# Two kinds of small copies in the ConvGLU stage move from ScalarE to VectorE

## The reference: what is computed

```
def conv_glu(h, prev, p):
    u = h @ p['w_up']                       # (rows, 2 * 2816)
    L = u.shape[1]
    pad = jnp.concatenate([prev, u], axis=1)
    c = p['conv_b'] + p['conv_w'][0] * pad[:, 0:L]
    for j in range(1, CONV_W):              # CONV_W = 3
        c = c + p['conv_w'][j] * pad[:, j:j + L]
    a, g = jnp.split(c, 2, axis=-1)
    return (jax.nn.silu(g) * a) @ p['w_down'], pad[:, -(CONV_W - 1):]
```

## Time and profile before

| what | value |
|---|---|
| median of 3 runs | 2471.32 us (2468.33 to 2472.02) |
| the profiled execution: its time | 2468.33 us |
| its span, first to last instruction | 2466.5 us |
| mean granted clock of TensorE | 0.981 |
| TensorE busy | 2352.0 us, 95% |
| VectorE busy | 1094.4 us, 44% |
| ScalarE busy | 990.8 us, 40% |
| POOL busy | 864.8 us, 35% |

### The profile page before, as it was taken

One profiled execution on the slowest core, in us unless ns is written; L12 is line 12 of the kernel. 1 busy time (PEld: TensorE's weight loads), 2 busy tenths in 40 slices (PEclk: granted clock), 3 DMA queues, 4 the chain that ended last, 5 costly groups with the idle time before them and its releaser, 6 DMA issues.

```text
span 2466.5 us, 48737 instructions
## 1 busy us (share of the span) xinstructions
PE 2352.0 (95%) x16832; PEld 2163.7 (88%) x16832; DVE 1094.4 (44%) x1676; ACT 990.8 (40%) x2052; POOL 864.8 (35%) x365
## 2 busy tenths in 40 slices
PE   5999999999999999999989999999999999999998
PEld 4888889999999997898778888899999989978986
DVE  3644463244452564266144544533353525633651
ACT  4544553234223553355244444532342234533542
POOL 3243132235333343344342342232353324434433
PEclk9999999999999899999989999999999999999999
DMA  4132212322222221322212122222122223213322
GB/s 133 62 99 81 69 61 72 97 67 67 84 72 86 70 82 65 94 80 82 82 62 87 61 81 82 72 76 85 60 71 75 81 70 86 76 63 97 86 78 89
DMA packets 239156, 193.52 MB, mean 78 GB/s; under 512 B 7088, under 2 KB 225296, under 8 KB 238960
## 3 DMA queue, kind: packets, MB, share of 16 engines
q1 hardware_dynamic: 217552, 172.38, 22.7%
q10 hardware_dynamic: 21408, 18.55, 2.3%
HBM read 177.49 MB, written 13.42 MB: 77 GB/s over the span
## 4 chain that ended last, share of the span: by engine, by line
issue 65%; POOL 17%; PE 12%; DVE 4%; ACT 2%; POOLq 1%; DVEq 0%; ACTq 0%
POOL wlo L509 13%; POOL rstd L515 3%; PE ps L968 2%; PE ps L614 2%; PE ps L969 2%; PE ps L616 2%; PE ps L970 2%; PE ps L615 2%; DVE ca L1926 2%; PE ps L659 1%; DVE ca L1931 1%; ACT ca L1373 1%; PE ps L960 0%; PE ps L959 0%; DVE ca L1936 0%
## 5 line engine op out<-in xcount | busy, mean ns | idle before, releaser
L509 POOL TENSOR_TENSOR wlo<-raw,whi 128x1024 fp32r<-128x1024 f32 (+2 forms) x322 | 773.4, 2424 | 1518.4 <-ACT whi L1002 1518.4
L614 PE MATMUL ps<-hl,whi 128*128 128x272 f32 x2240 | 650.8, 291 | 8.2 <-DVE mer L1861 4.8
L616 PE MATMUL ps<-hl,wlo 128*128 128x272 f32 x2240 | 646.7, 289 | 0.0
L615 PE MATMUL ps<-hl,whi 128*128 128x272 f32 x2240 | 644.8, 288 | 0.0
L631 PE MATMUL ps<-whi,hl 128*128 128x256 f32 x1792 | 516.5, 288 | 1.7 <-issue 1.0
L632 PE MATMUL ps<-wlo,hl 128*128 128x256 f32 x1792 | 509.0, 284 | 0.0
L633 PE MATMUL ps<-whi,hl 128*128 128x256 f32 x1792 | 508.0, 284 | 0.0
L614 PEld LDWEIGHTS ps<-hl,whi 128*128 128x128 f32 x2240 | 423.9, 189 | 11.8 <-DVE mer L1861 5.0
L616 PEld LDWEIGHTS ps<-hl,wlo 128*128 128x128 f32 x2240 | 422.9, 189 | 0.0
L615 PEld LDWEIGHTS ps<-hl,whi 128*128 128x128 f32 x2240 | 422.5, 189 | 0.0
L1002 ACT ACTIVATE whi<-raw 128x1024 fp32r<-128x1024 f32 (+2 forms) x322 | 311.8, 1016 | 237.2 <-PE ps L970 137.0
(11 more groups left out here) (215 smaller groups left out, 3024.1 us busy)
## 6 DMA issues: line engine op xcount, KB each, us to landing
raw<-in_w_in_dram SPq DMA_DIRECT2D x130, 512.0 KB, 4.6
raw<-in_w_up_dram SPq DMA_DIRECT2D x88, 512.0 KB, 4.8
raw<-in_w_branch_a_dram SPq DMA_DIRECT2D x16, 512.0 KB, 3.9
raw<-in_w_branch_b_dram SPq DMA_DIRECT2D x16, 512.0 KB, 4.4
raw<-in_w_out_dram SPq DMA_DIRECT2D x16, 512.0 KB, 3.9
raw<-in_w_down_dram SPq DMA_DIRECT2D x32, 256.0 KB, 3.8
raw<-in_w_down_dram SPq DMA_DIRECT2D x16, 512.0 KB, 3.7
raw<-in_w_down_dram SPq DMA_DIRECT2D x8, 768.0 KB, 4.5
```

The lines of the kernel that those rows point to most:

```text
L509: ins = e.tensor_tensor(wlo[:, s, a:b], raw[:, s, a:b], whi[:, s, a:b].bitcast(F32), ALU.subtract)
L614: e.matmul(out, wh, hi, start=(c == 0), stop=False)
L615: e.matmul(out, wh, lo, start=False, stop=False)
L616: ins = e.matmul(out, wl, hi, start=False, stop=(c == KC - 1))
```

## The change

`last_rows` and `state_rows` go from ScalarE's program. VectorE makes the same copies with `tensor_copy`: the state columns of unit 0 at the head of the pass, and in every unit, after L1931 and before the wait for tanh, the two last-row copies of unit j and the two state copies of unit j + 1. The waits follow: TensorE's transposes wait for VectorE, ScalarE's first tap waits for VectorE's state copies, and ScalarE's L1432 waits for VectorE's last-row copies of unit j - 2 and no longer for its own instruction before; VectorE's L1915 no longer waits for ScalarE's last-row copies.

```
 def conv_rows():
     acquire("t", dve=1)
-    e.wait_ge(*S.at("act_step", ("cs", FB - 1)))
+    e.wait_ge(*S.at("dve_step", ("cs", FB - 1)))
...
 # ScalarE
         if s == 0:
-            e.wait_ge(*S.at("dve_step", "edges"))
+            e.wait_ge(*S.at("dve_step", ("pads", j)))
...
-    def last_rows(j):
-        e.wait_ge(*S.at("dve_free_" + UP_BANKS[j % 2][3], ("ug", j, 1)))
-        for q in range(2):
-            c0 = SEQ if q == 0 else TOK + 2
-            e.wait_ge(*S.own())
-            e.activation(cs[:, 2 * q:2 * q + 2, :]..., up[:, j % 2, :, c0:c0 + 2], ACT.Copy)
-    def state_rows(j):
-        if j >= 2:
-            e.wait_ge(*S.at("dve_step", ("conv2", j - 2, 1)))
-        for s in range(2):
-            e.wait_ge(*S.own())
-            e.activation(up[:, j % 2, s, SEQ + 2:SEQ + 4], conv[...], ACT.Copy)
...
-    state_rows(0)
-    state_rows(1)
     for j in range(FB):
         ...
             first_tap(j - 1, 1)
-            last_rows(j - 1)
             half_tanh(j - 1)
-            if j + 1 < FB:
-                state_rows(j + 1)
         e.wait_ge(*S.at("mm_ready", ("T", j, 0, 0)))
         if j >= 2:
+            e.wait_ge(*S.at("dve_step", ("cs", j - 2)))
             e.wait_ge(*S.at("dve_step", ("conv2", j - 2, 1)))
-            e.wait_ge(*S.own())
...
     first_tap(FB - 1, 1)
-    last_rows(FB - 1)
     half_tanh(FB - 1)
 # VectorE
+    def pads(j):
+        for s in range(2):
+            e.wait_ge(*S.own())
+            e.tensor_copy(up[:, j % 2, s, SEQ + 2:SEQ + 4],
+                          conv[:, ds(l, 1), 0:2, ds(f * FB + (j + s * FT), 1)].rearrange("p a v c -> p (a v c)"))
+    pads(0)
     for j in range(FB):
         for t in range(2):
             e.wait_ge(*S.at("mm_ready", ("T", j, 1, t)))
-            if t == 0 and j >= 2:
-                e.wait_ge(*S.at("act_step", ("cs", j - 2)))
...
         # after the two L1931
+        for q in range(2):
+            c0 = SEQ if q == 0 else TOK + 2
+            e.wait_ge(*S.own())
+            e.tensor_copy(cs[:, 2 * q:2 * q + 2, :].rearrange("p t (s c) -> p s t c", s=2)[:, :, :, j],
+                          up[:, b, :, c0:c0 + 2])
+        if j + 1 < FB:
+            pads(j + 1)
         e.wait_ge(*S.at("act_step", ("th", j)))
```

More of the change, by code:

```diff
@@ L1374, in first_tap @@
                             *S.up("act_step", key=("tap0", j, s)))
-                    def last_rows(j):
-                        e.wait_ge(*S.at("dve_free_" + UP_BANKS[j % 2][3], ("ug", j, 1)))
-                        for q in range(2):
-                            c0 = SEQ if q == 0 else TOK + 2
-                            e.wait_ge(*S.own())
-                            e.activation(cs[:, 2 * q:2 * q + 2, :].rearrange("p t (s c) -> p s t c", s=2)[:, :, :, j],
-                                         up[:, j % 2, :, c0:c0 + 2], ACT.Copy).then_inc(*S.up("act_step", key=("cs", j) if q else None))
-                    def state_rows(j):
-                        if j >= 2:
-                            e.wait_ge(*S.at("dve_step", ("conv2", j - 2, 1)))
-                        for s in range(2):
-                            e.wait_ge(*S.own())
-                            e.activation(up[:, j % 2, s, SEQ + 2:SEQ + 4],
-                                         conv[:, ds(l, 1), 0:2, ds(f * FB + (j + s * FT), 1)].rearrange("p a v c -> p (a v c)"),
-                                         ACT.Copy).then_inc(*S.up("act_step", key=("pads", j) if s else None))
                     def half_tanh(j):
@@ L1903, in dve_program @@
                     e.wait_ge(*S.own())
-                    e.memset(up[:, :, :, 0:2], 0.0).then_inc(*S.up("dve_step", key="edges"))
+                    e.memset(up[:, :, :, 0:2], 0.0).then_inc(*S.up("dve_step"))
+                    def pads(j):
+                        for s in range(2):
+                            e.wait_ge(*S.own())
+                            e.tensor_copy(up[:, j % 2, s, SEQ + 2:SEQ + 4],
+                                          conv[:, ds(l, 1), 0:2, ds(f * FB + (j + s * FT), 1)].rearrange("p a v c -> p (a v c)")).then_inc(
+                                *S.up("dve_step", key=("pads", j) if s else None))
+                    pads(0)
                     for j in range(FB):
@@ L1933, in dve_program @@
                                 *S.up("dve_step", key=("conv2", j, 1) if v == 2 else None))
+                        for q in range(2):
+                            c0 = SEQ if q == 0 else TOK + 2
+                            e.wait_ge(*S.own())
+                            e.tensor_copy(cs[:, 2 * q:2 * q + 2, :].rearrange("p t (s c) -> p s t c", s=2)[:, :, :, j],
+                                             up[:, b, :, c0:c0 + 2]).then_inc(*S.up("dve_step", key=("cs", j) if q else None))
+                        if j + 1 < FB:
+                            pads(j + 1)
                         e.wait_ge(*S.at("act_step", ("th", j)))
```

## The result

The changed kernel takes 2485.27 us (median of 5 runs, 2481.79 to 2486.53) and the kernel before 2471.32 (5 runs). The ratio is 1.0056, with a 95% interval from 1.0045 to 1.0067: slower by 14 us. The profiled execution has a span of 2482.8 us, 16.3 more than before.

What follows compares the result with a forecast made beforehand. Stage F's ScalarE-VectorE round, longer than TensorE's 12.0 us a unit, bounds the pass. Copies needing 1.06 us in a 0.98 us hole cost 40 x 0.08 = +3.2 us on 2471.3, forecasting 2474.5 us; range 2466 to 2485.

Steps and rivals of the forecast that it cites:

- the sum for the four copies on VectorE: Between L1931 and L1936: copies and gaps need 1.06 us in a hole of 0.98, late by 0.08 a round, +3.2 us.
- Gain 0: ScalarE's removed state copies L1391, 0.76 us per j, lie beside VectorE's L1936 and L1942, so removing them changes nothing.
- What bounds the kernel: Stage F: the ScalarE-VectorE round, averaging 12.75 us, exceeds TensorE's 12.0 a unit, so TensorE waits before the down projection.
- The gains of nothing: On ScalarE: removing copies L1382 (0.45 us per j) and L1391 (0.76 us per j) gains 0 each.
- the reading that L1931 was not waiting for it: VectorE's L1931 starts 0.37 us after the first tap, before the second copy L1382 is over; the profile's naming is attribution.
- My upper bound: VectorE's four copies cost what they cost on ScalarE: 1.29 us, late by 0.31 a round, +12.4 us, 2484.
- such hiccups: Delays of 0.3 to 0.4 us in a few rounds may move when code is added, 2 to 3 us either way.
- The second one, clearly slower: VectorE copies cost as on ScalarE, or wait registers cannot load meanwhile: late 0.12 us or more a round, 2481 to 2484; 28%.
- The clock: Before the down projection: longer waits shift TensorE's slow-clock stretch by a few matmuls, under 2 us over all passes, no term.

Runs made afterwards that it cites:

- e6: Kernel before, with POOL's subtraction of stage F cut in four instructions a unit and not two: 2436.58 us, ratio 0.9867.
- e1: Changed kernel with only the last-row copies moved to VectorE, the state copies staying on ScalarE: 2471.18 us, ratio 0.9999 to before.
- e3: Changed kernel with neither engine making the last-row or state copies: 2476.54 us, ratio 1.0027 to before.
- e2: Changed kernel with only the state copies moved to VectorE, the last-row copies staying on ScalarE: 2475.89 us, ratio 1.0019 to before.
- e5: Kernel before, ScalarE untouched, with four more copies on VectorE at the change's place, into unused buffers: 2478.13 us, ratio 1.0035.
- e8: Changed kernel with the two state copies moved to VectorE's next wait, for ScalarE's copy L1403: 2473.96 us, ratio 1.0008 to before.
- e4: Changed kernel with all four VectorE copies put earlier, into its wait for the first tap of half 1: 2521.31 us, ratio 1.0199 to before.
- e11: Changed kernel with state copies moved to VectorE's wait for L1403, and POOL's stage F subtraction cut in four: 2443.28 us, ratio 0.9889 to before.
- e7: Changed kernel with POOL's subtraction of stage F cut in four instructions a unit: 2468.75 us, ratio 0.9999 to before.

## Why the prediction was wrong

Two steps failed: the sum for the four copies on VectorE, late by 0.08 us a round in the prediction and by 0.32 when measured, and the "Gain 0" for taking L1391 from ScalarE, which was a loss of 0.26 us a round.

**What bounds the kernel: right.** Stage F's round against TensorE's 12.0 us, the lag caught up with at unit 10, 40 rounds that count. Time and mean round go together in nine kernels, and once the round is down to TensorE's 12.0 us the waits vanish (e6).

**The gains of nothing: right for L1382** (e1), and the reading that L1931 was not waiting for it. **Wrong for L1391.** The prediction says "Gain 0" of taking them away, and counts ScalarE's copies by their time alone. They also worked out the address that the first taps use. Without them each first tap is 0.13 us later, +0.26 us a round (e3), less the 0.08 us that VectorE is quicker before L1931 (plain round +0.17 in e2, 7 us). VectorE is 0.09 us quicker before the other half too, but there the next instruction waits for POOL's and gives it back: 2.78 us for 2.68. This term was missing from the sum.

**The sum on VectorE: mis-sized.** I had "2 x (0.035 + 0.147) + 2 x (0.17 + 0.147) + 0.05", 1.05 to 1.06. Measured: the pair of last-row copies 0.03 + 0.38, then 2 x (0.21 + 0.17), then 0.12 to L1925: 1.30. Three parts are larger than I took them: the copies are 0.17 us and not 0.147 (worked out from a copy of one element, 144 ns, and one of 32 in a row, 180, which reads PSUM and not SBUF); the gap before the state copies is 0.21, where the register instruction lasts 129 ns; and behind the last short copy 0.12 us pass, not 0.05. So the hole was overfilled by 0.32 us and not 0.08. My upper bound, ScalarE's own cost, gave 0.31, and this is what VectorE cost. The term alone is 12.8 us; e5 has it by itself (plain round 0.32 - 0.08 = 0.24 expected, 0.26 measured), and e8 shows the same copies free where they fit. The table that the Trainium skill has for VectorE ("VectorE: DVE Perf Modes", on the TRN2 errata) was further off: by an estimate from its 58 cycles 64 ns, against 170. By the same estimate its remark of about 150 cycles gives 156 ns, which is near.

**What went the other way.** The plain round grew 0.49 us (0.32 + 0.26 - 0.08), 19.6 us over 40 rounds, but the mean only 0.37, 14.8 us. The kernel before loses 0.12 us a round on average to irregular delays (rounds of 13.04 and 12.93 between those of 12.58, the same ones in every pass), and the changed kernel next to none. I had named such hiccups as worth 2 to 3 us either way; they were worth 4.8. In the trace of before one VectorE instruction starts about 0.36 us late in each of two rounds of every pass, though what it waits for comes no later: L1947 after 1.35 us of idle time for 0.98, and the first L1926 after 0.80 for 0.45. Why this comes and goes with the code is open; no run was made for it.

**The rivals.** The second one, clearly slower, was what happened, by its first wording and for another reason as well. I gave it 28% and its price as 2481 to 2484; the measured 2485.27 lies 0.3 us above my range. That it came so near is luck: the overfilled hole alone gave 2478.13 (e5), and both causes without the lost delays would have given some 2491, as an estimate from the 19.6 us. The clock: TensorE's busy time grew by 2.6 us, a little over the "under 2 us" I allowed.

## What to carry to other kernels

Before work is moved to an idle engine, find the loop of hand-overs that sets the pace and measure each hole in it: here 0.98 us of idle time covered two of the four small copies, but not all four, which need 1.30, and both engines were under half busy. An instruction with a computed address also does address work for the ones after it; taking it away can put that work behind a wait, and the count of register instructions at the next lines shows it in the trace. A small copy on VectorE beside a long POOL instruction can cost the length of that instruction, so look at what POOL does at the new place, and consider cutting its instructions if VectorE is on the path: that gave 34 us in the kernel before, but only some 16 in the changed one, whose copies then came to lie beside POOL.

## What the runs showed of the hardware

- A VectorE copy of 2 to 4 elements between SBUF operands takes 0.17 us, and 0.21 us pass before it where its address is computed; ScalarE's takes 0.20 us and 0.18. For such copies VectorE is no cheaper.
- A VectorE copy of two or four elements, one input, waits for a running POOL instruction: 1.88 us for a pair in place of 0.38 (e4), up to 2.37 us for one in place of 0.17 (changed kernel, head of a pass).
- POOL's subtraction in four instructions of 512 columns and not two of 1024 took 1.3% off the kernel before when done in one stage and 1.6% in all; the two are not clearly apart.
- One program can run in two ways, by whether the weight split waits for TensorE or not: e11 has rounds of 12.1 us in the first part of each pass and of 12.5 and more behind it. Two different programs stay in one of them: e6 at 12.0, e7 at 12.8.
